# Modulation weights: 48 of 96 tiles moved out of two busy stages into the four norms, as batches of 12, 14, 14 and 8

## The reference

```
cond_lat = jax.nn.silu(c)[:, None, :]
cond_ctx = jax.nn.silu(c_ctx)[None, None, :]
for i in range(DEPTH):
    mod_l = split_cols(cond_lat @ w_mod[i] + b_mod[i], (D_MODEL,) * 6)
    mod_c = split_cols(cond_ctx @ w_mod[i] + b_mod[i], (D_MODEL,) * 6)
    a_lat = modulate(rmsnorm(h_lat, norm1_g[i]), mod_l[0], mod_l[1])     # shift 0, scale 1
    h_lat = h_lat + mod_l[2] * o_lat                                      # gate 2, after the mixer
    f_lat = modulate(rmsnorm(h_lat, norm2_g[i]), mod_l[3], mod_l[4])     # shift 3, scale 4
    h_lat = h_lat + mod_l[5] * peer_ffn(f_lat, ...)                       # gate 5
```

## Time and profile before

| | |
|---|---|
| median of three runs | 5144.19 us |
| profiled execution | 5136.25 us, span 5134.5 us |
| PE busy | 4354.7 us, 85% |
| DVE busy | 3454.5 us, 67% |
| ACT busy | 1211.8 us, 24% |
| POOL busy | 1806.3 us, 35% |

### The profile page before, as it was taken

How to read it: one execution, slowest core, us unless ns; L and a number is a source line. 1 busy time by engine, 2 the same in 40 slices (tenths; PEclk the granted TensorE clock), 3 DMA queues, 4 the chain that set the end, 5 groups by cost and what they waited for, 6 DMA issues and landing times. The chain is left out here.

```text
span 5134.5 us, 54423 instructions
## 1 busy us (share of the span) xinstructions
PE 4354.7 (85%) x18847; PEld 2969.3 (58%) x18847; DVE 3454.5 (67%) x7226; ACT 1211.8 (24%) x2191; POOL 1806.3 (35%) x1652
## 2 busy tenths in 40 slices
PE   7899976693888799999999977886737778999997
PEld 5676664381555466666666644552523435666665
DVE  2366665478888877776777746765688775666665
ACT  2222311210443311111111123331203332222221
POOL 0022121023666555554555500000226764334431
PEclk9899988796999999999999989997869889999998
DMA  6967776513998999999999927667228999999995
GB/s 232 313 187 213 206 211 171 192 49 133 356 373 334 344 366 355 362 354 345 371 356 358 356 90 208 187 192 229 98 98 323 334 345 350 355 355 358 357 357 193
DMA packets 514327, 1407.98 MB, mean 274 GB/s; under 512 B 45692, under 2 KB 128636, under 8 KB 509214
## 3 DMA queue, kind: packets, MB, share of 16 engines
q1 hardware_dynamic: 329758, 733.60, 43.9%
q0 software_dynamic: 184320, 671.17, 34.4%
HBM read 1226.33 MB, written 178.26 MB: 274 GB/s over the span
## 5 line engine op out<-in xcount | busy, mean ns | idle before, releaser
L1666 POOL DMA_INDIRECT expert_rows<-u_rows,peer_arena x640 | 878.8, 1373 | 1330.6 <-DVE expert_rows L1940 1069.4
L1711 PE MATMUL ps<-part_arena,peer_part_arena 128*128 128x384 f32 (+1 forms) x4096 | 1035.7, 335 | 32.4 <-DVE peer_part_arena L1983 30.5
L1940 DVE SCALAR_TENSOR_TENSOR expert_rows<-expert_rows,mixer_in 128x1024 f32<-128x1024 f32 x640 | 759.7, 1219 | 120.9 <-DMA expert_rows<-u_rows,peer_arena 117.7
L1683 PE MATMUL ps<-expert_rows,peer_arena 128*128 128x512 f32 x1024 | 536.1, 676 | 331.3 <-DVE peer_arena L1948 331.2
L1673 POOL DMA_INDIRECT expert_rows<-in_peer_v,peer_arena x640 | 724.2, 1132 | 195.3 <-issue 183.1
L1711 PEld LDWEIGHTS ps<-part_arena,peer_part_arena 128*128 128x128 f32 x4096 | 699.2, 190 | 95.3 <-issue 80.4
L1720 PE MATMUL ps<-best,peer_arena 128*128 128x512 f32 x1540 | 685.3, 592 | 0.0
L1711 PE MATMUL ps<-mixer_in_parts,peer_part_arena 128*128 128x384 f32 (+1 forms) x2048 | 633.3, 309 | 0.0
L1683 PEld LDWEIGHTS ps<-expert_rows,peer_arena 128*128 128x128 f32 x1024 | 211.5, 216 | 600.7 <-issue 307.3
L1967 DVE SCALAR_TENSOR_TENSOR peer_arena<-expert_rows,peer_arena 128x1024 f32<-128x1024 f32 x381 | 489.4, 1285 | 28.8
L2037 DVE TENSOR_TENSOR peer_arena<-peer_arena 128x384 f32<-128x384 f32 (+1 forms) x256 | 125.5, 490 | 494.1 <-ACT peer_arena L1849 494.1
(11 more groups left out here) (253 smaller groups left out, 6226.5 us busy)
## 6 DMA issues: line engine op xcount, KB each, us to landing
peer_arena<-in_peer_u SPq DMA_DIRECT2D x256, 512.0 KB, 8.4
best<-in_peer_v SPq DMA_DIRECT2D x154, 512.0 KB, 6.2
mixer_arena<-in_peer_u SPq DMA_DIRECT2D x272, 256.0 KB, 7.6
u_rows<-mixer_arena SPq DMA_DIRECT2D x136, 512.0 KB, 6.7
hidden<-in_peer_u SPq DMA_DIRECT2D x240, 256.0 KB, 6.4
u_rows<-hidden SPq DMA_DIRECT2D x120, 512.0 KB, 5.0
gates<-peer_arena SPq DMA_DIRECT2D x20, 2048.0 KB, 11.0
peer_arena<-in_peer_v SPq DMA_DIRECT2D x52, 512.0 KB, 6.2
```

The lines of the kernel that those rows point to most:

```text
L1666: pool.indirect_dma_start(u_ring[:, k % U_SLOTS, :], None, u_table, bass.IndirectOffsetOnAxis(u_index[s][:, m:m + 1], 0)).then_inc(u_row_i ...
L1683: mm = pe.matmul(ps[:, 2 + half, :], diag[m % V_SLOTS], v_ring[:, m % V_SLOTS, half * 512:half * 512 + 512], start=m == 0, stop=m == PAIRS ...
L1711: mm = pe.matmul(ps[:, 6, 0:dense_tok], left[j % len(left)][:, c, :], right[:, c, :], start=at == 0, stop=at == len(todo) - 1)
L1940: dve.scalar_tensor_tensor(out=rows, in0=rows, scalar=1.0, in1=B.x[:, :, rows_at + s * P:rows_at + s * P + P], op0=ALU.mult, op1=ALU.mult, ...
```

## The change

Each of the four norms gets a batch of modulation tiles: 12 in the norm in front of GLA, 14 in the norm in front of PEER of layer 0, 14 in the norm in front of attention and 8 in the norm in front of PEER of layer 1. A batch has an own buffer for all its tiles. Its three transfers (tiles 0 to 1, 2 to 5, and the rest) are the first thing that SP starts in the stage, ahead of the next stage's weights. PE multiplies them behind the sums of squares; in the two norms in front of PEER the last eight tiles are multiplied one by one behind the transposes of the eight column blocks. DVE adds the bias at the end of the stage. GLA keeps 12 tiles, three a head, at steps 1, 3 and 5 of the backward phase; `peer` of layer 0 keeps 20, in its first 20 lots.

```diff
+MOD_START, MOD_NORM, MOD_GLA, MOD_PEER = 2 * C, (12, 14, 14, 8), 12, 20
+MIXER_AHEAD = (18600, 13440)
...
+        ends = [MOD_START + MOD_NORM[0], MOD_START + MOD_NORM[0] + MOD_GLA + MOD_NORM[1]]
+        ends += [ends[1] + MOD_PEER + MOD_NORM[2], DEPTH * 6 * C]
+        tiles = [(end - n, n) for end, n in zip(ends, MOD_NORM)]
...
+class ModBatch:
+    def __init__(self, B, ar, first, count):
+        self.B, self.count = B, count
+        self.at = slice(first, first + count)
+        self.w = ar.take(count * C * P).rearrange("p (m c n) -> p m c n", m=count, c=C)
+        self.out = B.ps[:, 7, 0:2 * count].rearrange("p (m s) -> p m s", s=2)
+        self.ends = (2, 6, count)
+        self.landed, self.summed = [B.sem(f"tile_in{n}") for n in range(len(self.ends))], B.sem("summed")
+
+    def load(self, sp):
+        for n, end in enumerate(self.ends):
+            some = slice(self.ends[n - 1] if n else 0, end)
+            sp.dma_start(self.w[:, some].rearrange("p m c n -> p m (c n)"),
+                         self.B.a["w_mod"][self.at][some].rearrange("m p c n -> p m (c n)")).then_inc(self.landed[n], 16)
+
+    def multiply(self, pe, m):
+        if m == 0 or m in self.ends:
+            pe.wait_ge(self.landed[self.ends.index(m) + 1 if m else 0], 16)
+        for c in range(C):
+            mm = pe.matmul(self.out[:, m, :], self.w[:, m, c, :], self.B.cond[:, c, :], start=c == 0, stop=c == C - 1)
+        if m == self.count - 1:
+            mm.then_inc(self.summed, 1)
...
+    mod = ModBatch(B, ar, *tiles) if tiles else None
+    first_tiles = 0 if not mod else mod.count - C if split else mod.count
@@ norm, tensor
             mm.then_inc(used, 1)
+        for m in range(first_tiles):
+            mod.multiply(pe, m)
         if split:
             for c in range(C):
...
                 mm.then_inc(row_mm, 1)
+                if mod:
+                    mod.multiply(pe, first_tiles + c)
@@ norm, vector and sync
+        if mod:
+            mod.add(dve)
...
+        if mod:
+            mod.load(sp)
         if ahead:
             ahead(sp)
@@ gla
-    MOD = 4 * C // H
+    MOD = MOD_GLA // H
-                        mod.load(sp, MOD * h + m + 2, m % 2)
+                        mod.load(sp, MOD * h + m + 2, (MOD * h + m) % 2)
@@ peer
-    MOD = 6 * C
+    MOD = MOD_PEER
```

More of the change, by code:

```diff
@@ L219, in build @@
             keys = make(product_keys, layer, segs)
-            stages += [make(norm, layer, B.gains[:, layer], 0, 1, (CTX, LAT), 0, mixer["ahead"]),
+            stages += [make(norm, layer, B.gains[:, layer], 0, 1, (CTX, LAT), 0, mixer["ahead"],
+                            tiles[2 * layer]),
                        mixer, project,
-                       make(norm, layer, B.gains[:, 2 + layer], 3, 4, segs, SPARSE_TILES[layer], keys["ahead"]),
+                       make(norm, layer, B.gains[:, 2 + layer], 3, 4, segs, SPARSE_TILES[layer], keys["ahead"],
+                            tiles[2 * layer + 1]),
                        keys, make(peer, layer, segs)]
@@ L325, in add @@
                           self.B.mod_bias[:, at].unsqueeze(2).to_broadcast([P, tiles, 2]), ALU.add).then_inc(self.added, 1)
+class ModBatch:
[18 more added lines that the diff above has]
+            mm.then_inc(self.summed, 1)
+    def add(self, dve):
+        dve.wait_ge(self.summed, 1)
+        dve.tensor_tensor(self.B.mod.rearrange("p l k c s -> p (l k c) s")[:, self.at, :], self.out,
+                          self.B.mod_bias[:, self.at].unsqueeze(2).to_broadcast([P, self.count, 2]), ALU.add)
 class RowTurner:
@@ L430, in modulation, with norm @@
     return {"sync": sync, "tensor": tensor, "scalar": scalar, "vector": vector}
-def norm(B, layer, gain, shift, scale, segs, split=0, ahead=None):
+def norm(B, layer, gain, shift, scale, segs, split=0, ahead=None, tiles=None):
     dst = B.x
@@ L444, in norm @@
     factor = ar.take(C * 2).rearrange("p (c s) -> p c s", s=2)
+    if not split:
+        ar.at = MIXER_AHEAD[layer]
+    mod = ModBatch(B, ar, *tiles) if tiles else None
+    first_tiles = 0 if not mod else mod.count - C if split else mod.count
     used, squared, root, chain_s, scaled, shifted, high, low, row_mm, row_ev = (
@@ L562, in gla @@
     ps = B.ps
-    MOD = 4 * C // H
+    MOD = MOD_GLA // H
     BESIDE = [range(MOD * s // CHUNKS, MOD * (s + 1) // CHUNKS) for s in range(CHUNKS)]
-    mod = ModTiles(B, (ar, ar), "mod", 2 * C, 1, ps[:, 7, 0:2 * MOD])
+    mod = ModTiles(B, (ar, ar), "mod", MOD_START + MOD_NORM[0], 1, ps[:, 7, 0:2 * MOD])
     names = ("const_in", "w_in", "wv_in", "lo_mm", "lo_ev", "u_mm", "u_ev", "z_chain", "z_act", "la_ok", "passed",
@@ L743, in head @@
                 for m in BESIDE[s]:
-                    mod.multiply(pe, MOD * h + m, m % 2, m)
+                    mod.multiply(pe, MOD * h + m, (MOD * h + m) % 2, m)
                 if s < NB:
@@ L1566, in peer @@
     apart = y_tok[0][:, 0:LOT_ACT * P].rearrange("p (t k) -> p t k", t=LOT_ACT)
-    MOD = 6 * C
-    mod = ModTiles(B, (ar, Arena(y_tok[1])), "mod", 6 * C, 1, ps[:, 5, 0:2 * MOD]) if layer == 0 else None
+    MOD = MOD_PEER
+    mod = ModTiles(B, (ar, Arena(y_tok[1])), "mod", MOD_START + MOD_NORM[0] + MOD_GLA + MOD_NORM[1], 1, ps[:, 5, 0:2 * MOD]) if layer == 0 else None
     ar.at = at
```

## The result

The changed kernel takes 5161.15 us (median of eight runs, 5152.74 to 5169.31), the kernel before 5143.83 us in the same comparison (eight runs, 5140.47 to 5150.16): ratio 1.0035, 95% interval 1.0025 to 1.0045. It is 17 us slower; 23 were forecast.

The account below looks back on a forecast made before the run. Limits were taken by stage: serial norms, PE and DMA queue near their limit in GLA's backward phases, DVE in the gates' stretch. 84 + 1 - 50 - 12 = +23 us on 5144.2 gave 5167 us, range 5146 to 5186.

Parts of the forecast that it names:

- The clock in the norms, +84 us: Four norms: clock falls soon after the sums, tiles cost 3.41 us; norms grow 18.8, 19.9, 24.5 and 20.8 us.
- Rival 1: Norms: batches run at full 2.4 GHz clock, norms grow about 1, 0, 5 and 5 us; 5094 us, chance 0.07.
- GLA, -50 us: GLA's backward phases: 20 tiles removed, `level_sums` starts earlier, 12.5 us for each of four heads; bounds -28 and -66.
- Rival 2: GLA gives only what its turns give, -28 us in place of -50; 5189 us, chance 0.12.
- rival 3: GLA and gates' stretch both pay their upper bounds, -66 and -22 us; 5141 us, chance 0.12.
- The gates' stretch, -12 us: Layer 0's gates' stretch: 28 tiles removed, gain only in lots 20 to 31, 12 us; bounds 0 and 22.
- Rival 4: Gates' stretch is bound by bytes alone, 28 tiles give 40 us; 5139 us, chance 0.06.
- Semaphore clearing, +1 us: Norms: SP clears four more semaphores in each, first norm gets a new clearing; 1 us in all, between 0 and 4.

Follow-up runs that it names:

- the swapped form: Changed kernel with 12, 14, 12, 8 tiles; in norms before GLA and attention, conditioning is the weight block and 512 tile columns move: 5114.64 us, 0.9951 of before.
- The two experiments in GLA: Kernel before, GLA's 32 tiles: one of eight matmuls per tile done, 5118.64 us (0.9957); or only the first two tiles loaded, 5125.36 us (0.9971).
- the gates' stretch alone: Kernel before with batches of 14 and 14 in norms before layer 0's PEER and attention; GLA keeps 32 tiles, gates' stretch 20: 5171.09 us, 1.0058.

## Why the prediction was right, point by point

**The clock in the norms, +84 us.** Measured 79.2 in this profile. That tiles would run at the slow price in spite of an always busy PE, the step on which the sign hung, held: 3.41 us each and PEclk 0.50. Rival 1 is out as the prediction put it, an unbroken stream of these matmuls; the swapped form shows that its mechanism, PE at full clock through the batch, is to be had with another form. By the Trainium skill's rule ("TensorE: Matmul & The Clock Gate", Part 1: The HAM clock gate) activity releases the throttle. If the profile's busy time is taken for activity, the changed kernel's rows, with PE busy 10.00 of 10.00 us at 0.50, contradict the rule; the swapped form's, at 1.00, agree with it. The small error of the term is in the two norms with transposes: I added durations (0.87 + 3.41, 0.67 + 3.41) whose tails overlap. The fourth norm's rows show a period of 3.73 us (3639.30 to 3643.03), not 4.08; eight of them make 2.8 of the 3.1 us by which it was overstated. The second norm's rows show 3.95 us (960.75 to 964.70), not 4.28, which takes 2.7 us off; that +19.7 still came so near to +19.9 is luck, because in this profile the six tiles ahead of the transposes took 17.8 us and not 16.0, the clock falling sooner than I had it, and the sums 13.4 us and not 12.6. In the three other runs with this batch the norm grew by 16.5 us.

**GLA, -50 us.** Measured -49.1. The sum over the heads is nearer than its parts: I had 12.2 us for head 0 and some 12.5 for each, and the four heads gave 15.0, 9.8, 10.8 and 12.9. The two experiments in GLA bear out the reason to take the joint effect and not a sum of prices: one price away gives 11 us, both give 49. The turn of step 4 came 140.0 us behind the stage's start (147.2 before), 7.2 us earlier where I had 4.6: my 30.6 us for the new periods came from a sum that gives 36.9 us for the old ones with their five tiles, where the rows have 35.15. Taken as a difference, three tiles of 2.1 us are 6.3. Rival 2, the turns' own gain only, is out; rival 3's bound of -66 was not reached, and with only 8 tiles left GLA, at 696.6 us, came no nearer to it.

**The gates' stretch, -12 us.** This term was mis-sized: 7 us over all profiles, 3.4 in this one. I had taken half of DVE's idle time between lots 20 and 31. The place was right and the size was not: the waits for gathers shrank by 0.6 us here and by 4.8 with the gates' stretch alone, those at tile changes by 2.1 and 2.4, and gathers still hold DVE for 32.9 and 28.7 us. I think that the gathers wait for the 2 MB stores of gates, which stayed, but no run took those away, so that stays open. Rival 4, 40 us by bytes, is ruled out by the change of the gates' stretch alone.

**Semaphore clearing, +1 us.** The first norm began 0.6 us later, but over the twelve profiles it begins anywhere between 63.4 and 66.0 us, so this term is too small to read.

With this profile's norms and GLA and the mean of the gates' stretch the sum is 79.2 - 49.1 - 7 = +23 us. That it is the forecast's number is partly luck: the norms were overstated by 5 us, and so was the gain of the gates' stretch. The medians say +17, with an interval of +13 to +23. Means over all the profiles that have these batches, or none, give +76 for the norms (17.7, 16.9, 23.8 and 18.0 us), -50 for GLA and -7, together +19, so most of the 6 us is what this one profile has above the mean. The rest is within what untouched stages differ from one execution to the next, and is not traced further.

## What to carry to other kernels

Idle time on an engine is room for so much work at the price that the work has *there*, and for TensorE that price doubles or not with the clock granted at that place; take it from a row where the same instructions run alone, not from one where they stand between heavier ones. A product with a thin operand should have the thin side as the weight block and the long side moving: here that took 12 tiles from 38.5 to 20.8 us, nearly all of it by the clock. And when work is moved out of a stage, ask of both its prices (engine and transfer) whether the other hides the gain, and move only what fills the gap.

## What the runs showed of the hardware

A stream of float32 matmuls with 128x128 weights and two moving columns kept PE busy for 38.5 us, and PEclk fell from 1.00 to 0.50 some 2.6 us into it and stayed there; it also fell, and read 0.50, when each tile had a 128x512 matmul beside it. The same products with 128x2 weights and 512 moving columns kept 1.00 for the 20.8 us that they took, behind the same sums of squares. A record of the thin form came every 213 ns at 0.50 and every 112 ns at 1.00 in the first batch, and its weight loads lasted 333 and 192 ns, so weight loading, too, followed the clock.
